# Hyena stage of a hybrid trunk on one core: the spectrum in eight sets of two PSUM banks instead of four sets of four, and its last inverse moved behind the next filter's first products

## The reference

```python
def long_conv(u, hf, bias):
    seqlen = u.shape[1]
    uf = jnp.fft.rfft(u, n=2 * seqlen, axis=1)
    y = jnp.fft.irfft(uf * hf[None], n=2 * seqlen, axis=1)[:, :seqlen]
    return y + u * bias

def hyena(p, lp, rows, row_len):
    u = short_conv(...) + lp['hy_conv_b']          # (1, 2048, 3 x 1024)
    v, x1, x2 = jnp.split(u.astype(f32), 3, axis=-1)
    hf = hyena_filters(seqlen, lp)                  # filters of two orders, their spectrum
    z = x1 * long_conv(v, hf[:, 0], bias[0])
    z = x2 * long_conv(z, hf[:, 1], bias[1])
    return z * jax.nn.silu(p['z_b'].astype(f32))
```

## Time and profile before

| | us |
|---|---|
| median of 3 runs | 4779.01 (4778.39 to 4779.55) |
| the profiled execution's own time | 4773.03 |
| its span in the trace | 4771.3 |
| PE busy in the span | 4368.1 (92%) |
| DVE, ACT, POOL busy | 2423.3, 1284.1, 1771.5 |

### The profile page before, as it was taken

How to read it: one execution, slowest core, us unless ns; L and a number is a source line. 1 busy time by engine, 2 the same in 40 slices (tenths; PEclk the granted TensorE clock), 3 DMA queues, 4 the chain that set the end, 5 groups by cost and what they waited for, 6 DMA issues and landing times. The chain is left out here.

```text
span 4771.3 us, 70365 instructions
## 1 busy us (share of the span) xinstructions
PE 4368.1 (92%) x28046; PEld 2759.7 (58%) x28046; DVE 2423.3 (51%) x3474; ACT 1284.1 (27%) x2716; POOL 1771.5 (37%) x1480
## 2 busy tenths in 40 slices
PE   6799999999999999999969999788888884899998
PEld 6556544444445444444458888556566652676775
DVE  2465765533456778983146666455555553122221
ACT  3112121111212111111135555444454541000000
POOL 1221233332333343332379998332424242121211
PEclk6799999999999999999989999999999997999999
DMA  5323232233333333324277786545444446332320
GB/s 178 103 69 99 74 99 85 75 101 104 121 112 101 95 108 110 110 80 141 80 194 217 220 219 177 202 161 188 162 175 172 169 163 216 134 128 70 133 78 27
DMA packets 457848, 626.45 MB, mean 131 GB/s; under 512 B 125674, under 2 KB 353026, under 8 KB 442820
## 3 DMA queue, kind: packets, MB, share of 16 engines
q1 hardware_dynamic: 405684, 504.31, 32.9%
q0 software_dynamic: 25360, 100.67, 6.6%
q10 hardware_dynamic: 26496, 17.18, 1.1%
HBM read 404.54 MB, written 217.53 MB: 130 GB/s over the span
## 5 line engine op out<-in xcount | busy, mean ns | idle before, releaser
L1371 PE MATMUL proj_b<-shared_S,proj_tw 128*128 128x512 f32 x1920 | 849.7, 594 | 0.0
L1371 PE MATMUL proj_b<-shared_A,proj_wt 128*128 128x512 f32 x1280 | 590.3, 605 | 44.2 <-issue 26.2
L1371 PEld LDWEIGHTS proj_b<-shared_S,proj_tw 128*128 128x128 f32 x1920 | 361.3, 191 | 433.5 <-issue 433.1
L1371 PEld LDWEIGHTS proj_b<-shared_A,proj_wt 128*128 128x128 f32 x1280 | 247.6, 194 | 358.0 <-issue 339.4
L736 POOL TENSOR_TENSOR proj_tw<-proj_wt 128x512 f32<-128x512 f32 x80 | 111.9, 1398 | 910.2 <-PE proj_b L1371 875.4
L1371 PE MATMUL proj_b<-shared_A,proj_tw 128*128 128x512 f32 x640 | 289.8, 596 | 3.4 <-DVE proj_u L1045 3.4
L1371 PE MATMUL proj_b<-shared_S,proj_wt 128*128 128x512 f32 x640 | 291.1, 598 | 0.0
L2674 PE MATMUL mrg_b<-mrg_za,mrg_w_a 128*128 128x256 f32 x1024 | 233.7, 382 | 27.3 <-DMA mrg_w_o<-in_w_out_dram 27.3
L2674 PE MATMUL mrg_b<-mrg_yb,mrg_w_b 128*128 128x256 f32 x1024 | 231.5, 379 | 0.0
L2674 PEld LDWEIGHTS mrg_b<-mrg_za,mrg_w_a 128*128 128x128 f32 x1024 | 195.5, 192 | 57.4 <-issue 31.1
L2687 PE MATMUL mrg_b<-mrg_w_o,mrg_mt 128*128 128x512 f32 x512 | 221.9, 594 | 6.6 <-POOL mrg_mt L2560 6.6
(11 more groups left out here) (294 smaller groups left out, 8133.6 us busy)
## 6 DMA issues: line engine op xcount, KB each, us to landing
proj_wt<-in_w_in_dram POOLq DMA_DIRECT2D x80, 1024.0 KB, 6.0
delta_nv<-scratch_NV SPq DMA_DIRECT2D x144, 256.0 KB, 4.0
delta_kq<-scratch_KQ SPq DMA_DIRECT2D x128, 256.0 KB, 4.2
scratch_bounce_f<-fft_first SPq DMA_DIRECT2D x32, 1024.0 KB, 3.8
fft_yf<-scratch_bounce_f SPq DMA_DIRECT2D x32, 1024.0 KB, 5.7
scratch_bounce_i<-fft_yi SPq DMA_DIRECT2D x32, 1024.0 KB, 4.5
fft_second<-scratch_bounce_i SPq DMA_DIRECT2D x32, 1024.0 KB, 8.7
scratch_hy<-proj_tok SPq DMA_DIRECT2D x48, 512.0 KB, 2.6
```

What stands on the lines that cost most here:

```text
L1371: last = pe.matmul(bank[:, :], weights[:, k, :], aa[operand][:, k, :], start=(k == 0), stop=(k == KH - 1))
```

## The change

Each spectrum phase is cut into eight sets h of two banks. A bank of X, R or M now takes four matmuls, with row tile q and column tile q in the first bank and q + 2 in the second, so a set uses 8 of the 16 tiles of the array for each kind; `inverse` uses the same eight. `xs`, `pre` and `pim` have two buffers each, `yi` is used in halves with a semaphore for each. TensorE's order in a set is X(h), R(h), T(h + 1), I(h - 1), M(h). The last inverse, I(7), moves into the next step's `filters`, behind the `times` of pairs 0 and 1; in the last step it follows directly. ScalarE makes the decays of pair 0 before it empties I(7). SyncE writes eight pieces of 512 KB instead of four of 1024 KB, and reads filter rows 2 and 3 after pieces 0 and 2.

```diff
-        yd, xs, pre, pim = (second[:, 2048 * j:2048 * (j + 1)].rearrange("p (i x) -> p i x", i=4) for j in range(4))
+        yd, xs0, xs1, pre0, pre1, pim0, pim1 = (second[:, 1024 * j:1024 * (j + 1)].rearrange("p (i x) -> p i x", i=2) for j in range(7))
+        xs, pre, pim = (xs0, xs1), (pre0, pre1), (pim0, pim1)
...
# SyncE
-                    for c in range(4):
-                        if c < 2:
-                            filter_read(t, c + 2)
-                        read(sp, "I", t, 4 * c + 3)
-                        sp.dma_start(by_four(T["bounce_i"][t % 2], c), yi[:, :, :]).then_inc(i_written, 16)
-                    sp.wait_ge(i_written, 64 * (t + 1))
+                    for h in range(PAIR):
+                        read(sp, "I", t, 2 * h + 1)
+                        sp.dma_start(by_four(T["bounce_i"][t % 2], h, 4), yi[:, 4 * (h % 2):4 * (h % 2) + 4, :]).then_inc(i_written[h % 2], 16)
+                        if h in (0, 2):
+                            filter_read(t, h // 2 + 2)
+                    for i in range(2):
+                        sp.wait_ge(i_written[i], 64 * (t + 1))
...
# ScalarE
+                def first_decays(t):
+                    act.wait_ge(w_in, 48 * (t + 1))
+                    decay(t, 0, 0)
+                    decay(t, 0, 1)
+
                 def filters(t):
-                    act.wait_ge(w_in, 48 * (t + 1))
                     for p in range(PAIR + 1):
-                        if p < PAIR:
+                        if 0 < p < PAIR:
                             decay(t, p, 0)
                             decay(t, p, 1)
...
+                        empty_turn(t, 0)
+                        ready(act, "S", t, 0)
+                        wait(act, gated, 3 * t)
+                        act.activation(norm[:, :], bank("S", t, 0)[:, 0:CB], ACT.Sqrt, bias=eps[:, 0:1]).then_inc(emptied["act"], 1)
+                        for h in range(PAIR):
+                            empty_data_spectrum(t, h)
+                            if h + 1 < PAIR:
+                                empty_turn(t, h + 1)
+                            if h:
+                                empty_inverse(t, h - 1)
+                        if t + 1 < STEPS:
+                            first_decays(t + 1)
+                        empty_inverse(t, PAIR - 1)
...
# VectorE
+                        empty_turn(t, 0)
+                        read(dve, "S", t, 0)
+                        dve.reciprocal(norm[:, :], norm[:, :]).then_inc(normed, 1)
+                        for h in range(PAIR):
+                            products("R", pre, t, h)
+                            if h + 1 < PAIR:
+                                empty_turn(t, h + 1)
+                            products("M", pim, t, h)
...
# TensorE
                     for p in range(PAIR + 1):
                         if p < PAIR:
                             times(t, p)
+                        if p == 1 and t:
+                            inverse(t - 1, PAIR - 1)
                         if p:
                             transform(t, p - 1)
...
+                def tiles(kind, t, h, mat, src):
+                    out = [take(kind, t, 2 * h + j) for j in range(2)]
+                    for j in range(2):
+                        for q in range(4):
+                            last = pe.matmul(out[j][tile((q + 2 * j) % 4), :], mat[tile(q), tile(q)], src(j)[tile(q), :], start=True, stop=True)
+                        last.then_inc(filled, 1)
...
+                def inverse(t, h):
+                    out = [take("I", t, 2 * h + j) for j in range(2)]
+                    read(pe, "M", t, 2 * h + 1)
+                    for mat, src, st in ((mats["ib"], pre, True), (mats["ib_rot"], pim, False)):
+                        for j in range(2):
+                            for q in range(4):
+                                r = (q + 2 * j) % 4
+                                last = pe.matmul(out[j][tile(q), :], mat[tile(r), tile(r)], src[h % 2][tile(r), j, :], start=st, stop=not st)
+                            if not st:
                                 last.then_inc(filled, 1)
...
+                        turn(t, 0)
+                        energy(t)
+                        for h in range(PAIR):
+                            data_spectrum(t, h)
+                            filter_spectrum("R", t, h)
+                            if h + 1 < PAIR:
+                                turn(t, h + 1)
+                            if h:
+                                inverse(t, h - 1)
+                            filter_spectrum("M", t, h)
+                        if t + 1 == STEPS:
+                            inverse(t, PAIR - 1)
```

More of the change, by code:

```diff
@@ L1943, in hyena @@
                 use(*[("D", t, 12 + i) for i in range(4)])
[L1944 to L1952, removed]
+                use(("T", t, 0), ("T", t, 1), ("S", t, 0))
+                for h in range(PAIR):
+                    for x, n in (("X", h), ("R", h), ("T", h + 1), ("I", h - 1), ("M", h)):
+                        if 0 <= n < PAIR:
+                            use((x, t, 2 * n), (x, t, 2 * n + 1))
+                if t + 1 == STEPS:
+                    use(("I", t, N2 - 2), ("I", t, N2 - 1))
             if t + 1 < STEPS:
@@ L2254, in empty_out, with empty_turn, products @@
                         dve.tensor_copy(dst, bank("Z", cb, n)[:, :].rearrange("p (n t) -> p n t", n=4)).then_inc(emptied["dve"], 1)
[L2256 to L2265, removed]
-                            if i == 0 and s:
-                                ready(dve, "I", t, 4 * s - 1)
-                            dve.tensor_tensor(dst[:, i, :], bank(kind, t, 4 * s + i)[:, :], xs[:, i, :], ALU.mult).then_inc(emptied["dve"], 1)
+                def empty_turn(t, h):
+                    ready(dve, "T", t, 2 * h + 1)
+                    dve.tensor_copy(yd[:, 1, :], bank("T", t, 2 * h + 1)[:, :]).then_inc(emptied["dve"], 1)
+                def products(kind, dst, t, h):
+                    if h >= 2:
+                        ready(dve, "I", t, 2 * h - 3)
+                    for i in range(2):
+                        ready(dve, kind, t, 2 * h + i)
+                        read(dve, "X", t, 2 * h + i)
+                        dve.tensor_tensor(dst[h % 2][:, i, :], bank(kind, t, 2 * h + i)[:, :], xs[h % 2][:, i, :], ALU.mult).then_inc(emptied["dve"], 1)
                 filters(0)
@@ L2279, in _ @@
                         empty_data(t, 3)
-                        for s in range(4):
-                            empty_turn(t, s)
-                            if s == 0:
-                                read(dve, "S", t, 0)
-                                dve.reciprocal(norm[:, :], norm[:, :]).then_inc(normed, 1)
-                            products(t, s)
+                        empty_turn(t, 0)
[6 more added lines that the diff above has]
+                            products("M", pim, t, h)
                     if t + 1 < STEPS:
@@ L2361, in turn @@
                         last.then_inc(filled, 1)
-                def tiles(kind, t, s, mat, src):
-                    out = [take(kind, t, 4 * s + i) for i in range(4)]
-                    for step in range(4):
-                        for i in range(4):
-                            j = (i + step) % 4
-                            last = pe.matmul(out[i][tile(j), :], mat[tile(i), tile(i)], src(j)[tile(i), :], start=True, stop=True)
-                            if step == 3:
-                                last.then_inc(filled, 1)
@@ L2372, in spectrum @@
-                def spectrum(t, s):
-                    read(pe, "T", t, 4 * s + 2)
-                    read(pe, "T", t, 4 * s + 3)
-                    tiles("X", t, s, mats["fb"], lambda j: yd[:, j, :])
-                    pe.wait_ge(f_in[s % 2], 16 * (2 * t + s // 2 + 1))
-                    mine = lambda j: yf[:, s % 2, 2 * j:2 * j + 2, :].rearrange("p g c -> p (g c)")
-                    tiles("R", t, s, mats["fb_re"], mine)
-                    tiles("M", t, s, mats["fb_im"], mine)
-                def inverse(t, s):
-                    out = [take("I", t, 4 * s + j) for j in range(4)]
-                    read(pe, "M", t, 4 * s + 3)
-                    for mat, src, st in ((mats["ib"], pre, True), (mats["ib_rot"], pim, False)):
-                        for step in range(4):
-                            for j in range(4):
-                                i = (j + step) % 4
-                                last = pe.matmul(out[j][tile(i), :], mat[tile(j), tile(j)], src[tile(j), i, :], start=st, stop=not st)
-                                if step == 3 and not st:
-                                    last.then_inc(filled, 1)
+                def tiles(kind, t, h, mat, src):
[4 more added lines that the diff above has]
+                        last.then_inc(filled, 1)
@@ new lines, in data_spectrum, with filter_spectrum @@
+                def data_spectrum(t, h):
+                    read(pe, "T", t, 2 * h)
```

(7 more changed lines are left out.)

76 lines of the change are left out of this document (30 added, 46 removed).

## The result

The changed kernel took 4723.43 us (median of 4 runs, 4721.50 to 4727.94) against 4778.70 (4 runs, 4778.16 to 4779.55): a ratio of 0.9886, 95% interval 0.9868 to 0.9903, so 55 us faster. The profiled execution took 4721.99 with a span of 4720.2, 51.1 us less than the span before. The forecast was 4740, with its own range of 4722 to 4756: the direction and the mechanism were right, the gain was larger.

What follows compares the result with a forecast made beforehand. No engine is full: each set waits on itself because two uses of four banks fill PSUM. Terms - 44.1 + 5 + 0.5 = - 38.6 from 4779.0 gave 4740 us; own range 4722 to 4756, overall 4720 to 4780.

Steps and rivals of the forecast that it cites:

- A group costs two rounds however few its tiles: TensorE's 32 x 32 matmul groups: 8 matmuls on 8 tiles still take two rounds of 0.43 us each.
- A set costs 5.60: Spectrum phase: one two-bank set takes 5.60 us on TensorE, from a range of 5.50 to 6.50.
- VectorE and ScalarE are not the bound: Within a 5.60 us set VectorE has 3.1 us of work and ScalarE 2.7, so TensorE bounds the steady part.
- One bank written from four row tiles costs nothing: X, R and M: four row tiles write one bank at once, in different partitions, at no added time.
- The junction, 6.6 from M(7) to `transform`: Spectrum to filter phase: `transform` starts 6.6 us behind the start of M(7), 50.7 behind the first T.
- 5 us for the lower clock: Hole between I(7) and `transform`: the clock may fall there, 0.7 us for each of seven steps, 5 us taken off.
- The last step + 0.5: Last step, with no filter to hide behind: 0 to + 1 us, taken as + 0.5.
- - 44.1: First T to third hx: 54.35 us against 60.65, 6.3 us less for each of seven steps.
- 1 (load delay): Matmul groups: load delay of 0.2 us each remains, set 6.2 to 6.6, total about 4763 to 4776; chance 0.15.
- 2 (lower clock): Half-empty tile groups: the clock falls within them, set 7.3 us, total about 4820; chance 0.08.
- 3 (bank): Four matmuls of one bank go one after another: group 3.4 us, set 18, total 5380; chance 0.04.
- Rival 4, late filter rows: Filter-row read for sets 4 and 5, issued later, lands late: at most 5 us in three steps, 4755; chance 0.05.

Runs made afterwards that it cites:

- e5: Changed kernel with 4 instead of 8 matmuls in each X, R and M group, half the spectrum left out; 4731.2 us, ratio 0.9908 to before.
- e6: Changed kernel with odd sets on the eight tiles that even sets leave idle, M on its own semaphore; 4701.5 us, ratio 0.9851 to before.
- e3: Changed kernel with one buffer each for xs, pre and pim instead of two; 4793.0 us, ratio 1.0037 to before.
- e4: Changed kernel, but ScalarE makes the first decays behind its copies of I(7); 4769.6 us, ratio 0.9987 to before.
- r_changed: The changed kernel itself, unaltered, profiled a second time and timed again; 4723.9 us, ratio 0.9888 to before.
- e1: Changed kernel without its move: eight sets, last inverse at the spectrum phase's end, first decays behind its copies; 4763.4 us, ratio 0.9979 to before.
- e7: e6 with SyncE's filter-row reads ahead of pieces 0 and 2 and first decays ahead of the copies of I(6); 4690.2 us, ratio 0.9821 to before.
- e8: e7 with the next block's data loads issued behind piece 4 of the inverse instead of ahead of piece 0; 4684.7 us, ratio 0.9809 to before.
- e2: Kernel before, four sets of four banks, with only the move: last inverse later, first decays before its copies; 4714.5 us, ratio 0.9877 to before.

## Why the prediction was right, point by point

- *A group costs two rounds however few its tiles*: right, and shown by e5 and from the other side by e6.
- *A set costs 5.60*: 5.47. The sum without the allowance for late loads was 5.50; the 0.1 that I added does not exist with 8 tiles. The rule of the Trainium skill that I set beside it (TensorE: Matmul & The Clock Gate, "Architectural detail: the array is 16× 32×32, not 1× 128×128", a queue of 64 entries) agrees with the trace: the delay came where 64 instructions stood in front, and went with 32. That the queue is the cause is not shown, since the tiles in use were halved with the instructions. Six sets make 0.8 of it, and X(1) started at 6.7 instead of 7.0: M(7) at 43.0 for 44.1.
- *VectorE and ScalarE are not the bound*: right. That the double buffers "cost nothing" is right too, but e3 shows that without them all is lost.
- *One bank written from four row tiles costs nothing*: right. A group of 16 MATMULs, four row tiles in each of two banks, takes 1.06 us, the old one of 32 took 1.15. The rule of the Trainium skill that speaks against it (TensorEngine Tiling (Array Packing), "Gotcha 1: PSUM Pressure") would have made its start to the next 3.4 instead of 0.86; here the writers of a bank lie in different partitions, and the measurement decides.
- *The junction, 6.6 from M(7) to `transform`*: 6.57, by the path that was forecast: table load and decays stand in front of the copies of I(7), and e4 shows that this order is needed.
- *5 us for the lower clock*: none. All seven stretches are at 1.00, in r_changed too, with a hole of 1.67 ahead of `transform`. With 2.27 (e6) two of seven stretches are at 0.97, with 4.40 (e1) and 6.36 (e4) all are at 0.94 to 0.97, and with no hole there (e7) none lost clock there. So to watch this hole was right; it was short enough, which I had not reckoned out.
- *The last step + 0.5*: - 2.0. O waits 9.22 for its data, where it waited 11.52; I gave the smaller last piece too little and M(7) came 1.1 earlier.

```profile
3936.44 16.96 PE L2358 MATMUL fft_b<-fft_second,fft_ia 128*128 128x256 f32 x64 [9.22 <-DMA fft_second<-scratch_bounce_i]
```

The terms were - 44.1 + 5 + 0.5 = - 38.6; they measure - 52.0, 0 and - 2.0, and + 3.3 from outside. So the mis-sized terms are 1.1 us a step by the set and the start (7.9 in all), the clock (5.0) and the last step (2.5). The profiled executions differ by 51.0, the medians by 55.3, because the profiled one lay 5.7 below the median before and 1.4 after. The forecast had added 6.0 for this, so of the 17 us between 4740 and 4723.4 some 4.5 are no term of the sum but the spread of the runs.

Of the rivals, 1 (load delay), 2 (lower clock) and 3 (bank) did not come. Rival 4, late filter rows, was there but hidden: the reads landed in 11.0 at most, and only in step 2 one set took 5.70; a faster set laid it open (e6). Of the second rival's mechanism e5 shows a trace: with a quarter of the array at work the clock fell, but only behind a hole; with half of it, it did not fall within the groups unless TensorE had waited for a DMA (e7, step 2).

What I had not said, though my own sum held it (M(7) at 44.1, the last M before at 39.2): the eight sets lengthen the way to the last M, and all the gain is in the move, ScalarE's half of it included.

## What to carry to other kernels

Before you cut a stage finer so that engines overlap, price the finer piece on the busiest resource: 8 matmuls on 8 tiles cost TensorE as much as 16 on 16, and a busy share that rose from 70% to 98% brought 1.3 us a step. Look at what stands between two full phases: one table load and two decays in the wrong place in ScalarE's queue were worth 46 us in seven steps (e4 against the changed kernel; TensorE's half of the move is in both). If a piece must be small, put neighbours on the tiles that it leaves idle, and then look again at the transfers whose slack you have used up. With both, the small sets overtake the move alone (0.9821 in e7 and 0.9809 in e8 against 0.9877 in e2); the move alone with the orders of e7 and e8 was not tried.

## What the runs showed of the hardware

- 32 x 32 matmuls on different tiles do not start in program order: M, issued behind `ib_rot`, started its first MATMUL 0.24 us before `ib_rot` did (e6). What the order of their ends is, the trace does not tell, so M was given a semaphore of its own.
- The number of tiles at work had no effect on a round: 16 tiles 0.43 us (kernel before), 8 tiles 0.43 (changed kernel), 4 tiles 0.43 (e5).
- When X, R and M used a quarter of the array (e5), the lower clock came once in four of seven steps, 8.2 to 8.9 us behind the first T and just behind a hole of 0.84. When they used half, it came in the spectrum phase of no step of the changed kernel, e1, e3, e4, e6 and e8, and in one of e7, behind waits for a DMA.
- Over these kernels, the longer TensorE stood idle just ahead of the first `transform`, the more often `transform` ran at the lower clock: with no hole (e7, e8) in none of seven steps, with 1.67 us (changed kernel; 1.63 in e3) in none, with 2.27 (e6) in two, with 4.40 (e1) and 6.36 (e4) in all.
